# Differential attention on one core: TensorE takes the four transpositions of a quarter step before the scores

## The reference, cut to what matters

```python
def _diff_attention(q, k, v, lam):
    ...
    def block(qi):
        sc = jnp.einsum('bqhcd,bkhcd->bhcqk', qi, k, preferred_element_type=jnp.float32) * scale
        p = jax.nn.softmax(sc, axis=-1)
        w = p[:, :, 0] - lam * p[:, :, 1]
        return jnp.einsum('bhqk,bkhd->bqhd', w.astype(v.dtype), v)
```

## Time and profile before

| | us |
|---|---|
| median of 3 runs | 3015.54 (3011.91 to 3016.03) |
| profiled execution, its own time | 3021.86 |
| span of its profile, first to last instruction | 3020.1 |
| TensorE busy with matmuls | 2904.8 (96% of the span) |
| VectorE busy | 2144.5 (71%) |
| ScalarE busy | 1276.0 (42%) |
| mean granted clock of TensorE | 0.984 of 2.4 GHz |
| first score matmul of the attention starts at | 497.46 |
| last transposition of the attention starts at | 1143.32 (four, 1.11 long) |

### The profile page before, as it was taken

One profiled execution on the slowest core, in us unless ns is written; L12 is line 12 of the kernel. 1 busy time (PEld: TensorE's weight loads), 2 busy tenths in 40 slices (PEclk: granted clock), 3 DMA queues, 4 the chain that ended last, 5 costly groups with the idle time before them and its releaser, 6 DMA issues.

```text
span 3020.1 us, 39369 instructions
## 1 busy us (share of the span) xinstructions
PE 2904.8 (96%) x14244; PEld 2441.1 (81%) x14244; DVE 2144.5 (71%) x3092; ACT 1276.0 (42%) x2287; POOL 1394.9 (46%) x1100
## 2 busy tenths in 40 slices
PE   7999998999999998999899999999999999999997
PEld 3888886666666656888789999989999989999996
DVE  5666665988888865566766666677778676777768
ACT  3111113777777764456633333343333333333334
POOL 0233321011111125568745555585676566766754
PEclk9999999999999998999999999999999999999998
DMA  7444437021312105466532122242332224323213
GB/s 260 129 132 132 127 115 192 29 72 59 84 58 71 49 21 203 129 205 207 183 130 71 56 84 71 80 161 71 126 105 84 91 94 148 105 83 120 98 59 117
DMA packets 194061, 333.02 MB, mean 110 GB/s; under 512 B 15366, under 2 KB 102599, under 8 KB 193866
## 3 DMA queue, kind: packets, MB, share of 16 engines
q1 hardware_dynamic: 193868, 330.49, 34.1%
HBM read 250.72 MB, written 79.71 MB: 109 GB/s over the span
## 4 chain that ended last, share of the span: by engine, by line
PE 50%; POOL 4%; DVE 4%; DVEq 1%; DMA 1%; issue 1%; ACT 1%; POOLq 1%; SPq 0%; ACTq 0%
PE tail_bank L2336 9%; PE tail_bank L2338 9%; PE tail_bank L2337 9%; PE tail_bank L2365 5%; PE tail_bank L2367 5%; PE tail_bank L2366 5%; POOL tail_rounded L2066 2%; PE tail_bank L2269 1%; PE tail_bank L2271 1%; PE tail_bank L2270 1%; POOL tail_rounded L2076 1%; POOL tail_rounded L2082 0%; DMA tail_plain<-scr_h_d 0%; DVE tail_plain L2507 0%; PE tail_bank L2218 0%
## 5 line engine op out<-in xcount | busy, mean ns | idle before, releaser
L2066 POOL TENSOR_TENSOR tail_rounded<-tail_plain,tail_rounded 128x512 fp32r<-128x512 f32 x462 | 656.8, 1443 | 488.5 <-ACT tail_rounded L1838 488.3
L2336 PE MATMUL tail_bank<-tail_rounded 128*128 128x384 f32 x1848 | 622.2, 337 | 20.8 <-DVE tail_plain L2532 10.0
L2338 PE MATMUL tail_bank<-tail_rounded 128*128 128x384 f32 x1848 | 620.6, 336 | 0.0
L2337 PE MATMUL tail_bank<-tail_rounded 128*128 128x384 f32 x1848 | 620.5, 336 | 0.0
L1838 ACT ACTIVATE tail_rounded<-tail_plain 128x512 fp32r<-128x512 f32 x462 | 271.6, 621 | 379.7 <-DVE tail_plain L2508 182.6
L2532 DVE TENSOR_TENSOR tail_plain<-tail_plain,tail_bank 128x384 f32<-128x384 f32 x462 | 247.5, 548 | 254.8 <-PE tail_bank L2338 194.4
L2336 PEld LDWEIGHTS tail_bank<-tail_rounded 128*128 128x128 f32 x1848 | 349.4, 189 | 25.3 <-issue 21.0
L2337 PEld LDWEIGHTS tail_bank<-tail_rounded 128*128 128x128 f32 x1848 | 349.5, 189 | 1.3
L2338 PEld LDWEIGHTS tail_bank<-tail_rounded 128*128 128x128 f32 x1848 | 349.1, 189 | 0.0
L1154 DVE TENSOR_REDUCE att_peak<-att_sc 128x1 f32<-128x1024 f32 x256 | 312.6, 1221 | 42.1 <-PE att_sc L966 35.6
L2365 PE MATMUL tail_bank<-tail_rounded 128*128 128x512 f32 x792 | 310.8, 392 | 15.6 <-DVE tail_plain L2631 4.8
(11 more groups left out here) (287 smaller groups left out, 5139.9 us busy)
## 6 DMA issues: line engine op xcount, KB each, us to landing
tail_plain<-in_w_gu SPq DMA_DIRECT2D x132, 512.0 KB, 4.9
keep_ahead<-in_w_dn SPq DMA_DIRECT2D x66, 512.0 KB, 6.5
proj_ada<-in_w_ada SPq DMA_DIRECT2D x16, 1024.0 KB, 6.9
held_w_hi<-scr_qs_d SPq DMA_DIRECT2D x128, 128.0 KB, 2.8
scr_h_d<-tail_plain SPq DMA_DIRECT2D x63, 256.0 KB, 4.5
tail_plain<-scr_h_d SPq DMA_DIRECT2D x45, 256.0 KB, 4.3
proj_x_in<-in_x SPq DMA_DIRECT2D x18, 512.0 KB, 6.7
scr_att_d<-held_w_hi SPq DMA_DIRECT2D x36, 256.0 KB, 2.9
```

The source lines that it names most:

```text
L2066: nc.gpsimd.tensor_tensor(w_lo[:, j, :], operand(F, j), w_hi[:, j, :].bitcast(F32), ALU.subtract).then_inc(wlo_done, 1)
L2336: nc.tensor.matmul(dst, w_hi[:, j, cols], h_hi[j][:, k, :], start=(k == 0), stop=False)
L2337: nc.tensor.matmul(dst, w_hi[:, j, cols], h_lo[j][:, k, :], start=False, stop=False)
L2338: m = nc.tensor.matmul(dst, w_lo[:, j, cols], h_hi[j][:, k, :], start=False, stop=(k == 3))
```

## The change

In every quarter in which both are there, `turn_weights(C, g)` is issued before `scores(N, ...)`, no longer behind it. A quarter is T S V, with Y or Z behind it where there is one. Nothing else is changed: the other engines' orders, the semaphores, the buffers and all counts stay.

```diff
                 for g in range(4):
+                    if live(C) and g < w_items(C):
+                        turn_weights(C, g)
                     if live(N) and g % 2 < halves_of(N):
                         scores(N, g // 2, g % 2)
-                    if live(C) and g < w_items(C):
-                        turn_weights(C, g)
                     for m in range(QUADS):
                         if N in summed_at(m):
                             sum_values(m, 4 * (N - summed_at(m)[0]) + g)
```

## The result

The changed kernel takes 3088.81 us (median of 4 runs, 3087.38 to 3094.86), the kernel before 3013.72 in the same comparison: a ratio of 1.0248, 95% interval 1.0232 to 1.0264. It is slower by 75.1 us; the prediction said 3089, +73.5.

The account below looks back on a forecast made before the run. TensorE's queue was taken to set the attention's end. Loop +31.0, Y and Z +40.5, `variance` +1 and ends +1 gave +73.5 us: 3095 profiled, 3089 as median; its own range 3062 to 3108, widened to 3060 to 3114.

Parts of the forecast that it names:

- The loop: T, scores, maximum, exponential, copy, back to T: 4.89 us for two quarters, 9.78 a step, 62 steps, +31.0 us.
- Y and Z: T directly behind these turns on TensorE waits until ScalarE has read them: 1.50 us, 27 times, +40.5 us.
- The first rival: Only T's wait for the reading of Y and Z costs: +19 us, a median of 3035, chance 0.11.
- `variance`: On VectorE, in steps with it, two maxima distances sum to 4.90 and just fill the loop: +1 us, 0 to 4.
- the start: At step 2 T must wait for the first `weigh` before any score; together with step 64, +1 us.
- the 0.9 us a quad: In the kernel before, TensorE's loss in the attention: 37.40 us a quad measured against a floor of 36.5.
- The weight load: A T that waited loads weights only after the wait, 0.05 us each; loading ahead would save 8 us in all.
- The other rivals: Faster, 3003, chance 0.03; a further wait in the loop, 3120, 0.05; a lower TensorE clock, hundreds of us more, 0.02.

Follow-up runs that it names:

- the odd quarters alone: The kernel before, with T ahead of S only in quarters 1 and 3: 3095.25 us, ratio 1.0267.
- ScalarE's order: The changed kernel, but on ScalarE the copy of a quarter stands before that quarter's exponential: 3035.92 us, ratio 1.0074.
- the longer copy: The changed kernel with ScalarE's copy of quarters 0 and 2 cut into eight pieces of 64 columns: 3148.44 us, ratio 1.0432.
- The run with the value product between: The kernel before, with S V T instead of S T V in the 27 quarters behind a Y or Z: 3014.70 us, ratio 0.9988.
- the even quarters alone: The kernel before, with T ahead of S only in quarters 0 and 2: 3051.37 us, ratio 1.0119.

## Why the prediction came out right

**The loop.** Its terms were all there in the trace before, though no loop ran in it: 4.89 from rows, 4.91 measured. That it is the loop, and the exponential in it, was shown from three sides: by the odd quarters alone (4.93 from T to T), by ScalarE's order (steps of 8.7 to 8.9), and by the longer copy (2d a step).

**Y and Z.** 1.50 each, 27 times, and 1.50 to 1.52 measured. Right for this kernel, because the loop has no slack. It is not a constant of the place: with S first elsewhere the same T costs 1.41 or 0.94, and 0.92 comes back when S is put first only there. The first rival, in which only Y and Z cost, priced a quad at 38.8 and the whole at +19. It is not what the changed kernel does, but the run with the copy first comes near it: a quad of 38.8, the stretch +19.3, the median +23.7.

**The sum.** 62 x 9.82 + 27 x 1.50 = 649.3, measured 649.7. Not each of the 62 steps follows it: step 2 takes 8.89, step 6 10.39, step 34 12.00 instead of 11.69, which nearly cancels. The loop's term came out at 62 x 9.82 - 575.3 = 33.5 where I had 31.0. The small terms were off the other way and made up for it: `variance` cost nothing (2.58 + 2.33 = 4.91 just fits into the loop), where I added 1; the start cost 0.5 (15.96 before, 16.47 after, from the first maximum of all to that of step 2); and from step 64 to the last transpositions the kernel is 2.0 us shorter (51.9 before, 49.9 after), which I hadn't seen. The hit within 0.2 us is luck: the runs of the changed kernel alone scatter by 7. The range was also added up wrongly: its own terms give 3089 - 12 - 15 - 1 - 2 = 3059 and 3089 + 12 + 3 + 2 = 3106, not 3062 and 3108.

**What was wrong in the reasoning, without harm.** I wrote that TensorE's queue sets the end and called the 0.9 us a quad its loss. The run with the value product between, and the one with T first only behind Y and Z, show that behind a Y or Z VectorE's row of maxima ends last in the kernel before; covering T's wait there shortened the stretch by 0.6 us, where 27 x 0.29 would have been 8. And "closed loops" were looked for only through the copy: the even quarters alone make one through VectorE's `weigh`, 9.14 us long, hidden in the full change behind the 9.82.

**The weight load.** In the loop a T that waited reaches its value product 1.42 us later (840.41 to 841.83), one that did not 1.37 (842.68 to 844.05). The 0.05 is paid, as read from the earlier trace rows. The Trainium skill, "TensorE: Matmul & The Clock Gate", section "Architectural detail: the array is 16× 32×32, not 1× 128×128", states that TensorE's queue can pull weight loads ahead of matmuls in flight. The changed kernel's trace agrees for T's that wait for nothing, whose first load starts 0.42 before the matmul (842.26 and 842.68). That the rule would also save the 0.05 of a T whose own wait is still open was my reading of it, and the trace shows the opposite: there the load starts with the matmul, at 840.41.

**The other rivals.** No further wait came in (T's matmuls wait for a `weigh` twice, 0.4 us in all; its weight loads wait 23 times, 7.9 us, nearly all of it while earlier matmuls still run), and the granted clock stayed at 1.00 of 2.4 GHz, with TensorE idle for 0.78 us behind each Y and Z.

## What to carry to other kernels

When two engines with hand-written orders hand work to each other, follow the dependencies around until they come back to the instruction they started from, add up the links, and compare with the busiest engine's work in that time: a moved block changes which loops exist, also those through a third engine's fixed order. Put first on one engine what the other engine delivers first. And let two uses of a buffer that has no second one not follow each other directly: the engine then stands still while it is read out, here 1.4 us from turn to turn, of which at most 0.5 came back.

## What was not expected of the hardware

An activation of 128x64 on ScalarE takes 0.10 us from start to start (seven in 0.73 us) and 0.29 when it stands last, while the whole 128x512 takes 0.59: cutting a copy in eight costs 0.43 us, in two 0.06. And the third stage, the same instructions each time, took 1869 to 1877 us in the profiled executions, which is more than many of the effects one would like to read from a single span.
